# Hybrid attention and convolution block on one core: order of the projection's pairs, place of two splits, queue of the last stores

## What is computed

```
h = rmsnorm(x, pre_norm_w)
proj = h @ w_in                                     # 1024 x 6144
q, k, v, z_att, gb, gc, u, z_conv, g_att, g_conv = split(proj)
q, k = partial_rotary(q, positions), partial_rotary(k, positions)
att = diff_attention(q, k, v, positions, lam)       # 4 heads, each softmax1 - lam * softmax2
y_att = (rmsnorm(att, subln_w) * 0.8 * silu(z_att)) @ w_att_out
cv = gb * short_conv(gc * u, conv_w)                # 3 taps along the rows
y_conv = (cv * silu(z_conv)) @ w_conv_out
m = sigmoid(g_att + bias0) * y_att + sigmoid(g_conv + bias1) * y_conv
out = x + rmsnorm(m @ w_out, post_norm_w)
```

## Time and profile before

| | us |
|---|---|
| median of 3 runs | 1769.21 (1768.13 to 1770.48) |
| profiled execution | 1770.07 |
| its span | 1768.2 |
| PE busy | 1715.2, 97% |
| DVE busy | 1040.2, 59% |
| ACT busy | 658.6, 37% |
| POOL busy | 247.7, 14% |

### The profile page before, as it was taken

The page is one execution under the profiler, slowest core; times in us unless marked ns, Lnnn a source line. Parts: engine busy times, 40 slices in busy tenths (PEclk is TensorE's granted clock), DMA queues, the critical chain, the costliest instruction groups (busy, mean ns, idle before and its releaser), DMA issues.

```text
span 1768.2 us, 22837 instructions
## 1 busy us (share of the span) xinstructions
PE 1715.2 (97%) x8344; PEld 1434.0 (81%) x8344; DVE 1040.2 (59%) x2087; ACT 658.6 (37%) x1168; POOL 247.7 (14%) x178
## 2 busy tenths in 40 slices
PE   7999999998999998799999999999999999999998
PEld 6888888887888876688888887888888778888887
DVE  5538655646777885267767665767766453424242
ACT  5422333224332322244444554444454442323231
POOL 0000000365322330111101112111001040000000
PEclk9999999999999999999999999999999999999999
DMA  6547999653323245976665679658576875353532
GB/s 238 155 171 297 383 346 336 216 168 109 120 76 115 72 120 159 297 229 187 194 212 183 197 235 265 196 177 230 194 232 187 264 262 184 112 188 108 184 107 73
DMA packets 169436, 343.62 MB, mean 194 GB/s; under 512 B 16097, under 2 KB 61153, under 8 KB 163809
## 3 DMA queue, kind: packets, MB, share of 16 engines
q1 hardware_dynamic: 169314, 342.06, 61.1%
HBM read 230.84 MB, written 111.16 MB: 193 GB/s over the span
## 4 chain that ended last, share of the span: by engine, by line
PE 89%; DMA 4%; DVE 2%; SPq 2%; POOL 1%; issue 1%; ACT 1%; DVEq 0%; ACTq 0%
PE bank L1411 17%; PE bank L1234 14%; PE bank L1235 14%; PE bank L1236 14%; PE bank L1371 6%; PE bank L1316 4%; PE bank L1318 4%; PE bank L1319 4%; PE bank L1343 3%; PE bank L1344 3%; PE bank L1354 3%; DMA q_st<-qk_s 1%; SPq L806 1%; DMA gate_s<-gate_st 1%; PE bank L1391 1%
## 5 line engine op out<-in xcount | busy, mean ns | idle before, releaser
L1411 PE MATMUL bank<-ht,w 128*128 128x512 f32 x912 | 239.7, 397 | 2.2 <-DMA w<-split_s 2.2
L2162 DVE CUSTOM_DVE_ANT_0 e<-bank,zeros 128x512 f32<-128x512 f32 x192 | 124.9, 688 | 133.0 <-PE bank L1344 132.6
L1411 PEld LDWEIGHTS bank<-ht,w 128*128 128x128 f32 x912 | 168.1, 190 | 35.1 <-DMA w<-split_s 2.7
L1705 ACT ACTIVATE e<-e,nbias 128x128 f32<-128x128 f32 (+15 forms) x128 | 153.6, 1200 | 80.0 <-DVE nbias L2171 79.9
L1234 PE MATMUL bank<-ht,w 128*128 128x512 f32 x448 | 174.4, 389 | 0.3 <-issue 0.3
L1236 PE MATMUL bank<-ht,w 128*128 128x512 f32 x448 | 174.3, 389 | 0.0
L1235 PE MATMUL bank<-ht,w 128*128 128x512 f32 x448 | 174.3, 389 | 0.0
L1316 PE MATMUL bank<-ht,a_op 128*128 128x512 f32 x392 | 155.4, 396 | 16.3 <-DVE stage L1959 7.2
L1218 POOL TENSOR_SCALAR mask<-kc,qc 128x128 f32<-128x128 f32 (+3 forms) x64 | 87.6, 1369 | 581.2 <-DVE mx L2162 580.7
L1318 PE MATMUL bank<-ht,a_op 128*128 128x512 f32 x392 | 154.9, 395 | 0.0
L1319 PE MATMUL bank<-ht,a_op 128*128 128x512 f32 x392 | 154.6, 394 | 0.0
(11 more groups left out here) (187 smaller groups left out, 3432.1 us busy)
## 6 DMA issues: line engine op xcount, KB each, us to landing
w<-split_s SPq DMA_DIRECT2D x124, 512.0 KB, 4.9
raw<-in_w_in SPq DMA_DIRECT2D x56, 512.0 KB, 5.5
split_s<-piece SPq DMA_DIRECT2D x24, 1024.0 KB, 5.9
q_st<-qk_s SPq DMA_DIRECT2D x128, 128.0 KB, 4.9
gate_s<-gate_st SPq DMA_DIRECT2D x64, 256.0 KB, 5.5
ring<-gate_s SPq DMA_DIRECT2D x64, 256.0 KB, 3.3
ht_s<-ht SPq DMA_DIRECT2D x6, 2048.0 KB, 10.3
qk_s<-stage SPq DMA_DIRECT2D x48, 192.0 KB, 3.5
```

The source lines that it names most:

```text
L1411: mm = nc.tensor.matmul(bank[2 + u % 2][:], unit_weights(u)[:, term // 2, k, :], h_slot(bb, k)[:, term % 2, :], start=i == 0, stop=i == PE ...
L1705: nc.scalar.activation(e, e, ACT.Exp, bias=nbias[G % 2][:, h:h + 1], scale=SCALE, accum_out=esum[G % 2][:, h:h + 1]).then_inc(exp_done, 1)
L2162: nc.vector.tensor_tensor_reduce(e[:, c:c + wide], bank[(0, 1, 4)[o % 3]][:, 0:wide], mask[m % 2][:, 0:wide] if masked else zeros[:, 0:wid ...
```

## The change

1. A list `PAIR_ORDER` says which pair of tiles stands at each place: 0, 1, 2, 3, 10, 4, 5, 11, 6, 7, 8, 9, 12, 13. The two rotary pairs, 10 and 11, come behind the first and the second convolution group. Every wait, bank and stage goes by the place. `load_tables(1)`, the cosine and sine of the second half, moves from place 5 to place 2 in SP's program.
2. At the passage ACT and DVE run `split_a(6)` and `split_a(7)` ahead of `split_t(4)`.
3. The stores of X and Y leave SP's program. ACT issues them by a new function `store_rest`, for two blocks each time behind the two `put_out`. SP's loads close up, and the first two gate units' weights wait for P7 of Y where the stores had stood around them.

```diff
+PAIR_ORDER = (0, 1, 2, 3, 10, 4, 5, 11, 6, 7, 8, 9, 12, 13)
+def tile(q, x):
+    return 2 * PAIR_ORDER[q] + x
 SEQ = ([(p, b) for p in range(LINE) for b in (0, 1)]
-       + [(2 * q + x, b) for q in range(2, X) for x, b in ((0, 2), (1, 2), (0, 3), (1, 3))]
+       + [(tile(q, x), b) for q in range(2, X) for x, b in ((0, 2), (1, 2), (0, 3), (1, 3))]
...
+        def store_rest(eng, p, b):
+            st = stage_at(p, b)
+            eng.wait_ge(dve_done, done_at(p, b))
+            for lo, hi, row in segments(place_of(p)):
+                eng.dma_start(qk_s[tile_of(p) // 4, :, row:row + hi - lo, b * BLK:(b + 1) * BLK]
+                              .rearrange("s p e -> p s e"), stage[st][lo:hi]).then_inc(stored[st], 16)
...
             for q in range(2, X):
-                if q == 5:
+                if q == 2:
                     sp.wait_ge(ht_lo_done, 2 * NT + 16)
                     load_tables(1)
...
             load_k(Plan(True), 0, 0)
-            for q in (X, Y):
-                store_block(2 * q + 1, 3)
+            sp.wait_ge(proj_done, product_at(POS[Y, "P7"]))
             load_unit(0)
             load_unit(1)
-            for q in (X, Y):
-                store_block(2 * q + 1, 2)
...
             load_unit(2)
-            for q in (X, Y):
-                store_block(2 * q, 2)
             load_v(Plan(True), 0, 0)
             sp.wait_ge(proj_done, product_at(POS[X, "P3"] - 1))
             load_unit(3)
-            for q in (X, Y):
-                store_block(2 * q, 3)
...
             split_t(3)
             take_p1(1)
-            split_t(4)
             split_a(6)
             split_a(7)
+            split_t(4)
...
             for x, b in ((1, 3), (1, 2), (0, 2), (0, 3)):
                 for q in (X, Y):
-                    put_out(2 * q + x, b)
+                    put_out(tile(q, x), b)
+                for q in (X, Y):
+                    store_rest(act, tile(q, x), b)
```

More of the change, by code:

```diff
@@ L105 @@
 SEQ = ([(p, b) for p in range(LINE) for b in (0, 1)]
-       + [(2 * q + x, b) for x, b in ((0, 2), (1, 3), (1, 2), (0, 3)) for q in (0, 1)]
-       + [(2 * q + x, b) for q in range(2, X) for x, b in ((0, 2), (1, 2), (0, 3), (1, 3))]
-       + [(2 * q + x, b) for x, b in ((1, 3), (1, 2), (0, 2), (0, 3)) for q in (X, Y)])
+       + [(tile(q, x), b) for x, b in ((0, 2), (1, 3), (1, 2), (0, 3)) for q in (0, 1)]
+       + [(tile(q, x), b) for q in range(2, X) for x, b in ((0, 2), (1, 2), (0, 3), (1, 3))]
+       + [(tile(q, x), b) for x, b in ((1, 3), (1, 2), (0, 2), (0, 3)) for q in (X, Y)])
 AT = {pb: i for i, pb in enumerate(SEQ)}
@@ L171, in stored_to @@
 def stored_to(p, i):
-    last = max(AT[x, y] for x, y in SEQ if x < p)
+    last = max(AT[x, y] for x, y in SEQ if QK_P <= x < p)
     return NT // 4 + sum(stores_of(x) for x, y in SEQ[:last + 1] if stage_at(x, y) == i)
@@ L1302, in product @@
                     out, right = bank[base], ht[0][:, 4:8]
-                    pe.wait_ge(dve_done, done_at(2 * q - 3, 2) if q >= 2 else done_at(LINE - 2 + q, 0))
+                    pe.wait_ge(dve_done, done_at(tile(q - 2, 1), 2) if q >= 2 else done_at(LINE - 2 + q, 0))
                 elif x == "P4":
@@ L1308, in product @@
                     out, right = bank[base + 1], ht[1][:, 0:4]
-                    pe.wait_ge(dve_done, done_at(2 * q - 3, 3) if q >= 2 else done_at(LINE - 2 + q, 1))
+                    pe.wait_ge(dve_done, done_at(tile(q - 2, 1), 3) if q >= 2 else done_at(LINE - 2 + q, 1))
                 for k in range(4):
@@ L1668, in _ @@
                     split_a(i + j)
-                put_out(2 * q, 2)
+                put_out(tile(q, 0), 2)
                 split_a(i + 5)
-                put_out(2 * q + 1, 2)
+                put_out(tile(q, 1), 2)
                 split_a(i + 6)
-                put_out(2 * q, 3)
+                put_out(tile(q, 0), 3)
                 if q + 1 < X:
                     take_p1(q + 1)
-                put_out(2 * q + 1, 3)
+                put_out(tile(q, 1), 3)
             i = POS[X, LAST_TWO[0]] + A_SLOTS
```

46 lines of the change are left out of this document (23 added, 23 removed).

## The result

| | before | after |
|---|---|---|
| median, us | 1768.13 (1764.51 to 1770.48, 5 runs) | 1752.77 (1748.39 to 1754.09, 5 runs) |
| profiled execution | 1770.07 | 1748.39 |
| its span | 1768.2 | 1746.6 |

The ratio is 0.991, 95% interval 0.9889 to 0.9931: faster by 15.4 us of median. The two profiled executions differ by more, 21.7 us, because the one of after was the shortest of its five. So I had the changed kernel timed again beside the last experiments: 1753.25 (1752.57 to 1755.03, 5 runs), ratio 0.9911 (0.9897 to 0.9924), profiled execution 1755.03. With two profiles of after, a term can be told from what differs between two executions of one program.

A forecast was written before the change was run, and what follows sets the result against it. PE, busy 97% of the span, bounds the kernel, so only gaps can be won. 7.8 + 4.3 + 8.5 = 20.6 us off the profiled 1770.07 gives 1749.5, and 1748.6 as median; range 1743.5 to 1757.0.

The forecast's parts named there:

- Bound: Whole kernel: PE is busy 97% of the span, so an edit leaving PE's work alone can only win gaps.
- Passage: Gap before P6 of pair 0 and its half clock go, 0.4 us opens before P7: gain 7.8 us (6.5 to 8.2).
- the raw loads of pairs 2 and 3 follow splits and sums that come earlier too: Passage: last step, claiming that these loads come earlier as well; no size of its own.
- Pairs: Rotary pairs moved between convolution groups: gaps and half clock fall from 14.3 to 10.0 us, gain 4.3 us (1 to 6).
- for pair 9, which stands there now: Place 11: DVE's block comes 8.9 us after P3, leaving a 6.2 to 6.4 us gap before P5 of Y.
- Stores: Start of attention: stores through ACT's queue win 8.5 us (2.5 to 11.6) of 11.6 us of gaps and half clock.
- the two bounds: Store landing: one shared line, DVE starts at 731, 2.5 us won; own line with half, all 11.6 won.
- (a): Start of attention: stores no faster, one shared backlog, DVE starts at 731; 1754.6 us, chance 0.18.
- (c): Passage not freed: P6 waits for something else than its split, the 7.8 us stay; 1756.4 us, chance 0.05.
- (b): Pairs: rotary pairs bring their gaps along, each repeating 5.4 us, 18.8 in place of 14.3; 1757.4 us, chance 0.12.
- (d): Slower: a DMA issue on ACT costs far more than on SP; 1784 us at 2.0 us an issue, chance 0.03.
- (e): Better still: all 11.6 us at the start of attention and no gap at P7; 1744 to 1746 us, chance 0.10.

The follow-up runs named there:

- after_again: The changed kernel, nothing altered, timed again on the same chip as the last experiments: 1753.25 us, ratio 0.9911 to the kernel before.
- e2_order: The kernel before with the new pair order alone, and the tables loaded at place 2: 1768.04 us, ratio 0.9996.
- e3_stores: The kernel before with only the stores of X and Y on ACT's queue and SP's loads closed up: 1756.71 us, ratio 0.9938.
- e4: e3_stores, but SP's loads keep their old places in time, waiting where a store had stood: 1762.76 us.
- e5: The kernel before with SP's attention loads drawn forward, but the stores of X and Y on SP's queue behind them: 1766.98 us.
- f6: The changed kernel, POOL holding S3 and S4 of pairs 12 and 13 until DVE wrote block 3 of place 11's first tile: 1746.97 us.
- f1: The changed kernel with the split of P3 of the pair in place 11 ahead of U2 on ACT and DVE: 1747.60 us.

## Why the prediction was right, and where not

The forecast was 1748.6 with a range of 1743.5 to 1757.0; the median came at 1752.77, the profiled execution at 1748.39. Faster was right. The sum for the profile, 1749.5, is 1.1 us off, but that is luck: passage and pairs were set 5.4 us too high together and the stores 4.7 too low, and the profiled execution was the shortest of its ten. Against after_again the sum is 5.5 us off.

- **Bound: right.** PE's work stayed as it was (8344 matmuls; busy 1715.2 and 1708.2 us, with the mean granted clock at 0.992 and 0.996), and all that moved were gaps.
- **Passage, 7.8 predicted, 5.7 measured, below its range.** The gap went with its half clock, 8.3 us (8.2 predicted), and P7 has its new gap, 0.9 for the 0.4 taken. The step that failed is the last one: "the raw loads of pairs 2 and 3 follow splits and sums that come earlier too". They came 1.3 us earlier, with PE 7.7. The cost stands at P5 of pair 2, 1.4 us. Before did show it: the earlier trace rows have ACT's order at 439.69, and the blocks whose stores precede the load stand behind those splits.
- **The clock's part differs between executions.** The same gap of 5.4 to 5.5 us at the passage stands in e2_order and e3_stores, and yet they were 1.2 us ahead of before behind it. So the 2.75 us of half clock in the 8.2 are some 1.5 to 1.8 in others. Behind P5 of Y it is the other way: 1.7 us in before, 2.5 to 2.7 in e3, e4 and e5. Before's one trace overstates the passage by about a microsecond and understates the pairs by as much.
- **Pairs, 4.3 predicted, 1.0 measured (0.4 in after_again), at the lower edge of its range.** The 1.0 twice, and the 2.7 and its 1.7 gone, came as forecast (by the starts 1.2 twice, against 1.2, 2.9 and 1.7 gone). The step that failed is the 8.9 us "for pair 9, which stands there now". Place 11 is not pair 9's old place: there POOL forms S3 and S4 of two pairs at once, 6.2 us of sums beside DVE's steps. It took 11.6. The gap was 9.0 for 6.3, and the half clock behind it 2.1 for 1.7. e2 shows that this comes with the order alone. f6 shows what POOL costs there, 3.8 us. Not all of that is new: in before the split and the copy of pair 9 were long too, beside the sums of its own place, and only its taps ran alone.

```profile
615.09 1.48 DVE L2005 TENSOR_TENSOR a_op<-s,a_op 128x512 fp32r<-128x512 f32 x1 [0.44 <-ACT a_op L1611]
616.50 1.25 DVE L1976 COPY cu<-carry 128x2 f32<-128x2 f32 x1
617.78 0.49 DVE L1980 TENSOR_SCALAR tmp<-cu,conv_w 128x512 f32<-128x512 f32 x1
```

  So of the 2.7 us between 8.9 and 11.6 the two taps make 1.9. By the other 0.8 DVE was already late when they began. Its wait for S1 of pair 13 is a candidate, and f1, which takes that wait away, won 0.6; what makes up the 0.8 is not shown further.
- **Stores, 8.5 predicted, 13.2 measured, above its range of 2.5 to 11.6 (10.9 in after_again, within it).** The mechanism was right: e4 shows the queue's part, e5 that the loads alone do little. The size was set too low in three places. I took DVE's start 14.1 us behind the first gate unit, between the two bounds (11.1 the near one); it was 12.1, and its scores decided, not lam (10.4). The 1.8 us kept back for the first rounds of attention never came. And what could be won was not 11.6 us but 12.8 (e3): by the starts each gap cost about 0.16 us more than its idle time, and the half clock 2.7 where I read 2.2. The 28 issues cost ACT 15.1 us (4.12 + 3.04 + 3.91 + 4.00), where 18 were reckoned. The row that misled me was 285 GB/s at a share of 1.04: I took it for what the engines could move.
- **Rivals.** (a) and (c) did not come. (b) did not either: C22 has no wait. (d) had the wrong price, 0.54 us an issue. (e) came for the stores alone.
- **Median against profile.** "It stood 0.86 above the median" was carried over to the changed kernel. Its ten runs lie from 1748.4 to 1755.0, and the profiled one is the lowest. Two profiles of one kernel differ by 6.6 us, more than the sum's error of 1.1 or the median's of 4.2, so one profile cannot tell a good forecast from a lucky one.

## What to carry to other kernels

A duration read for a step holds for the neighbours it had: if a pair moves to another place, reckon its steps again beside what the other engines do there, above all DVE's steps beside GpSimd's. A DMA share of 1.0 with one queue is no proof that the engines are full; stores that someone waits for can go to a second queue. And when PE comes earlier, follow each load that its next steps need back to what stands ahead of it in its queue.

## What the runs showed of the hardware

- With a second queue at work the DMA engines moved 342 to 361 GB/s at a share of 0.95 to 1.02, where one queue gave 252 at 0.95 and 298 at 1.00. The loads on SP's queue got slower for it: the V slices landed in 17.4 us (12.9 before).
- A DVE copy of 128x2 took 1.25 us beside GpSimd's sums and 0.16 alone; a 128x512 tensor_scalar 1.47 and 0.49, a scalar_tensor_tensor 1.66 and 0.75, a split 1.54 and 0.69. GpSimd's own sums took 1.72 each there (3.45 for two) and 1.3 where DVE did little.
- By the starts of the matmuls a wait of PE costs 0.15 to 0.2 us more than the idle time in its row: 0.95, 2.14 and 6.80 for 0.79, 1.98 and 6.64, and 2.87 for 2.70.
